# Attention in steps of two units on one Trainium2 core: products on separate halves of the array, MLA's mask in spare contraction rows

## Chip, core and metric

One core of one Trainium2 chip (trn2). The metric is the device time of one launch in microseconds (us). TensorE is PE in the profile and its weight loads are PEld; DVE is VectorE, ACT is ScalarE, POOL is GpSimd, SP is SyncE, which issues most DMAs.

## What is computed

One inference step of a layer with two head groups, for a prompt of 512 tokens and for 8 decoding sequences ("samples") of 16 new tokens with 256 cached ones. After the attention come the output projection and a retrieval layer (PEER) over 16,384 experts, which the change does not touch.

```python
def _attend(q, k, v, q_pos, k_pos, c_q, c_k, chunk_causal):
    s = jnp.einsum('bqhd,bkhd->bhqk', q, k, preferred_element_type=F32) * scale
    if c_q is not None:                      # FoX: 8 heads of 64
        s = s + (c[query] - c[key])
    if chunk_causal:                         # MLA: 8 heads of 64 + 32 rope
        mask = (k_pos[None, :] // CHUNK) <= (q_pos[:, None] // CHUNK)    # CHUNK = 64
    else:
        mask = k_pos[None, :] <= q_pos[:, None]
    s = jnp.where(mask, s, -jnp.inf)
    p = jax.nn.softmax(s, axis=-1)
    return jnp.einsum('bhqk,bkhd->bqhd', p.astype(v.dtype), v)
```

## The kernel before, in words

Everything is float32 with few exceptions (bf16 for masks and the FoX bias). The program runs through: norm and projections, transposes and MLA's up-projections, the attention stage, the output projection (L1012), PEER's queries and key scores, top-k and gate matrix, and a dense loop over 128 blocks of experts (L1117, L1133 to L1135), which takes the second half of the time.

The attention stage works on **units**. A prompt unit is one head and one tile of 128 queries, with the (i + 1) x 128 keys up to that tile; there are 32 of MLA and then 32 of FoX, ordered by pair of heads c, head hh and tile i. Between them stand 16 sample units, for each sample b one of FoX (all 8 heads x 16 queries as 128 rows, 272 keys) and one of MLA. The list `plan` (L350 to L357) writes the order out; each engine runs through it with its own lag. For a unit n:

- `scores` (L905, PE): the products into bank n % 3 of PSUM. MLA: one product over 96 rows (L924) and the mask of the diagonal block, added as identity times mask (L925). FoX: one over the head's 64 rows (L920), the bias (L921), the mask (L922). A FoX sample: four products over 128 rows, with zeros in qbd where a head doesn't belong, summed in one bank (L937), then bias and mask (L938, L939). An MLA sample: L941, L942.
- `row_max` (L1245, DVE), `exponentials` (L695, ACT), `normalise` (L1250, DVE, one unit later).
- `transpose_probabilities` (L945, PE, two units later): 128x128 blocks, into bank 3 + n % 2; `copy_transposed` (L703, ACT) brings them to SBUF.
- `values` (L955, PE, three units later): a prompt unit's products write 64 PSUM rows, the head's half (L966); a FoX sample's are 12 products with 32 moving columns (L982), an MLA sample's 3 with 128 (L985).
- `copy_out` (L1257, DVE, four units later).

So PE's program is scores(n), transposes(n - 2), values(n - 3), and so on, in order. What it waits for: scores wait for the exponentials of unit n - 3 (`exp_done`, the bank), transposes for the copy of unit n - 2 (`pt_copied`), values for their own copy.

```python
for n in range(ALL + 3):
    if n < ALL:
        scores(n)
    if 2 <= n < ALL + 2:
        transpose_probabilities(n - 2)
    if n >= 3:
        values(n - 3)
```

SP loads the caches of sample b into slot b % 2 once sample b - 2 has been used (`load_batch`, L422), w_o in between (L443). POOL writes the rope key rows of kmT (L513), zeroes and fills qbd (L516, L521), and then copies each sample's new keys (L538). After the stage, L998 up-projects the MLA samples' latents, head by head, to alternating halves of PSUM rows.

Of the kernel before, what the change touches and what calls it, by code (L numbers as in the profile page):

```python
# [36 lines left out]
P = 128  # L37
# [41 lines left out]
def peer_step_kernel(nc, t_in, t_out):  # L79
# [16 lines left out]
    with ExitStack() as ctx:  # L96
# [8 lines left out]
        eps_col = r("eps_col", [P, 8])  # L105
        late_at = r.at
# [205 lines left out]
        new_keys = sem("new_keys")  # L312
# [49 lines left out]
        def unit(n):  # L362

            m = plan[n][1]
            pair, hh, i = m // 8, m // 4 % 2, m % 4
            return 1 - pair // 4, pair % 4, hh, i, (i + 1) * P

        def keys_of(n):
            return unit(n)[4] if is_prompt(n) else L

        def batch_read(b):

            return place["sample", 2 * b + 1] + 1
# [10 lines left out]
        def _(sp):  # L384
# [54 lines left out]
            mla_read = place["prompt", UNITS // 2 - 1] + 1  # L439
            for b in range(DB):  # L440
                if b >= 2 and batch_read(b - 3 if b > 2 else 0) <= mla_read < batch_read(b - 2):
                    sp.wait_ge(pv_done, mla_read)
                    ld(w_o[:], t_in["w_o"]).then_inc(wo_loaded, 16)  # L443
                load_batch(b)
# [55 lines left out]
        def _(pool):  # L500
# [11 lines left out]
            for h in range(MH):  # L512
                nc.gpsimd.tensor_copy(kmT[64:96, h, :].rearrange("p (t k) -> p t k", t=TP),  # L513
                                      zT[64:96, 0:TP, 3, :]).then_inc(kr_copied, 1)
                pool.wait_ge(kr_copied, h + 1)
            link(nc.gpsimd.memset(qbd[:], 0.0))  # L516
            pool.wait_ge(proj_copied, 23)
            for c in range(4):
                for hh in range(2):
                    rows = slice(64 * hh, 64 * hh + 64)  # L520
                    nc.gpsimd.tensor_copy(qbd[rows, c, :, 2 * c + hh, :],  # L521
# [85 lines left out]
        def _(act):  # L607
# [87 lines left out]
            def exponentials(n):  # L695
                nk = keys_of(n)
                act.wait_ge(max_ready, n + 1)
                if n >= 4:
                    act.wait_ge(pt_done, n - 3)
                A(prob[:, n % 4, 0:nk], ps[:, n % 3, 0:nk], ACT.Exp, bias=small[:, 32 + n % 4:33 + n % 4],  # L700
                  accum_out=small[:, 36 + n % 4:37 + n % 4]).then_inc(exp_done, 1)

            def copy_transposed(n):  # L703
                act.wait_ge(pt_done, n + 1)
                if n >= 3:
                    act.wait_ge(pv_done, n - 2)
                bank = ps[:, 3 + n % 2]
                if is_prompt(n):
                    nk = keys_of(n)
                    A(probT[:, n % 3, 0:nk], bank[:, 0:nk], ACT.Copy).then_inc(pt_copied, 1)  # L710
                else:
                    A(probT[:, n % 3, 0:PAST], bank[:, 0:PAST], ACT.Copy)
                    A(probT[0:DS, n % 3, PAST:PAST + P], bank[0:DS, PAST:PAST + P], ACT.Copy).then_inc(pt_copied, 1)
# [110 lines left out]
        def _(pe):  # L824
            mm, tr = nc.tensor.matmul, nc.tensor.transpose
            identb, fmask, mmask, nmask = cb[:, 0:P], cb[:, P:2 * P], cb[:, 2 * P:3 * P], cb[:, 3 * P:3 * P + DS]
# [78 lines left out]
            def scores(n):  # L905
                bank = ps[:, n % 3]
                if n >= 3:
                    pe.wait_ge(exp_done, n - 2)
# [3 lines left out]
                if n == place["prompt", UNITS // 2]:  # L912
                    pe.wait_ge(nc_ready, 1)
                if is_prompt(n):
                    kind, c, hh, i, nk = unit(n)
                    h = 2 * c + hh
                    diag = bank[:, i * P:(i + 1) * P]
                    if kind == 0:
                        rows = slice(64 * hh, 64 * hh + 64)
                        mm(bank[:, 0:nk], fqT[rows, c, i * P:(i + 1) * P], kT[rows, c, 0:nk], start=True, stop=False)  # L920
                        mm(bank[:, 0:nk], selh[0:96, h], nc3[0:96, 0:nk], start=False, stop=False)  # L921
                        mm(diag, identb, fmask, start=False, stop=True).then_inc(s_done, 1)  # L922
                    else:
                        mm(bank[:, 0:nk], qmT[0:96, h, i * P:(i + 1) * P], kmT[0:96, h, 0:nk], start=True, stop=False)  # L924
                        mm(diag, identb, mmask, start=False, stop=True).then_inc(s_done, 1)  # L925
                    return
                b, kind = divmod(plan[n][1], 2)
                s = b % 2
                if kind == 0:
                    pe.wait_ge(batch_loaded[s], 16 * 7 * (b // 2 + 1))  # L930
                    pe.wait_ge(new_keys, 3 * (b + 1))
                    if b == 0:
                        pe.wait_ge(qbd_ready, 8)
                        pe.wait_ge(ncs_ready, 1)
                        pe.wait_ge(qs_ready, 3)
                    for c in range(4):
                        mm(bank[:, 0:L], qbd[:, c, b].rearrange("p h q -> p (h q)"), kTs[:, s, c], start=(c == 0), stop=False)  # L937
                    mm(bank[:, 0:L], selb[0:64, b], ncS[0:64], start=False, stop=False)  # L938
                    mm(bank[:, PAST:L], identb, nmask, start=False, stop=True).then_inc(s_done, 1)  # L939
                else:  # L940
                    mm(bank[:, 0:L], qps[:, b].rearrange("p h q -> p (h q)"), ckTs[:, s], start=True, stop=False)  # L941
                    mm(bank[:, 0:L], qrs[64:96, b].rearrange("p h q -> p (h q)"), krTs[64:96, s],  # L942
                       start=False, stop=True).then_inc(s_done, 1)

            def transpose_probabilities(n):  # L945
                pe.wait_ge(p_ready, n + 1)
                if n >= 2:
                    pe.wait_ge(pt_copied, n - 1)
                nk = keys_of(n)
                for c in range((nk + P - 1) // P):  # L950
                    w = min(P, nk - c * P)
                    last = tr(ps[0:w, 3 + n % 2, c * P:(c + 1) * P], prob[:, n % 4, c * P:c * P + w], ident[:])  # L952
                last.then_inc(pt_done, 1)

            def values(n):  # L955
                pe.wait_ge(pt_copied, n + 1)
                pT = probT[:, n % 3]
                if is_prompt(n):
                    kind, c, hh, i, nk = unit(n)
                    pair = plan[n][1] // 8  # L960
                    if plan[n][1] % 8 == 0 and pair >= 2:
                        pe.wait_ge(o_copied, pair - 1)
                    rows = slice(64 * hh, 64 * hh + 64)
                    for k in range(i + 1):
                        v = (fv, vm)[kind][:, k, (2 * c + hh) * 64:(2 * c + hh + 1) * 64]
                        last = mm(ps[rows, 5 + pair % 2, i * P:(i + 1) * P], v, pT[:, k * P:(k + 1) * P],  # L966
                                  start=(k == 0), stop=(k == i))
# [609 lines left out]
```

## Time and profile before

| | |
|---|---|
| median of 3 runs | 2066.52 us (2062.34 to 2066.69) |
| the profiled execution's own time | 2057.58 us |
| its span in the trace | 2055.7 us |
| PE busy over the span | 1875.9 us (91%) |
| DVE, ACT, POOL busy | 1565.2, 779.7, 913.9 us |
| mean granted TensorE clock | 0.93 |

Busy time is the union of an engine's instructions; the granted clock is given in shares of 2.4 GHz. A line such as `L966` is a line of the kernel, `128*64` the stationary operand (rows x columns), `128x128` the moving one. A float32 product shows as two instructions, a transpose as one. The duration of one instruction holds its latency too, so what a row of them costs is read from start to start.

### The profile page before, as it was taken

The numbers are of one execution on the slowest core, as the hardware profiler recorded it, in microseconds if no ns is written. First come the engines' busy times: TensorE is split into PE (matmuls) and PEld (weight loads), VectorE is DVE, ScalarE is ACT, GpSimd is POOL, SyncE is SP. The second block draws the span as 40 slices with busy tenths as digits, with TensorE's granted clock in tenths as the row PEclk, the third lists the DMA queues.
The fourth block names the chain that finished last, engine by engine and source line by source line (L and its number), as shares of the span: only waits on it lengthen the run. The fifth ranks groups of instructions, "written<-read, shape, count | busy, mean of one in ns | idle before, by whom it ended". The sixth has DMA issues, their size and how long they took to land.

```text
span 2055.7 us, 28703 instructions
## 1 busy us (share of the span) xinstructions
PE 1875.9 (91%) x9135; PEld 1519.7 (74%) x9135; DVE 1565.2 (76%) x3265; ACT 779.7 (38%) x1298; POOL 913.9 (44%) x727
## 2 busy tenths in 40 slices
PE   6999999999989952665799999999999999999998
PEld 4883666664555642664799999999999999999997
DVE  4314333332267989996799999999999999999999
ACT  4322432220211112995344344443444344443443
POOL 0011000000004445001477777777777777777772
PEclk8999877779999875999999999999999999999999
DMA  6110212102111002445899999999999999999994
GB/s 235 42 61 0 82 55 112 52 1 114 41 41 42 21 1 80 176 181 205 327 415 407 397 408 405 409 403 399 414 413 397 394 399 417 416 392 413 405 413 194
DMA packets 159300, 502.54 MB, mean 244 GB/s; under 512 B 17776, under 2 KB 51504, under 8 KB 155536
## 3 DMA queue, kind: packets, MB, share of 16 engines
q0 software_dynamic: 73728, 268.47, 32.7%
q1 hardware_dynamic: 85520, 233.42, 29.5%
q8 instruction: 27, 0.44, 0.1%
q14 instruction: 25, 0.20, 0.0%
HBM read 470.99 MB, written 30.84 MB: 244 GB/s over the span
## 4 chain that ended last, share of the span: by engine, by line
PE 84%; DVE 12%; ACT 2%; issue 1%; DMA 1%; SPq 0%; DVEq 0%; ACTq 0%
PE ps L1117 25%; PE ps L1133 9%; PE ps L1134 9%; PE ps L1135 9%; PE ps L1036 6%; DVE asel L1417 4%; PE ps L1012 3%; PE ps L966 3%; DVE bsel L1409 3%; PE ps L854 2%; PE ps L855 2%; PE ps L856 2%; PE ps L920 2%; PE ps L982 2%; PE ps L952 2%; PE ps L1043 1%
## 5 line engine op out<-in xcount | busy, mean ns | idle before, releaser
L543 POOL DMA_INDIRECT vbuf<-in_peer_v,ix x256 | 381.0, 1488 | 221.6 <-DMA gate_matrix<-stage 143.9
L543 POOL DMA_INDIRECT ubuf<-in_peer_u,ix x256 | 383.3, 1497 | 156.0 <-POOL ix L598 108.9
L1133 PE MATMUL ps<-hh,uh 128*128 128x384 f32 x1024 | 346.2, 338 | 10.7 <-DVE ul L1158 10.7
L1134 PE MATMUL ps<-hl,uh 128*128 128x384 f32 x1024 | 345.0, 337 | 0.0
L1135 PE MATMUL ps<-hh,ul 128*128 128x384 f32 x1024 | 344.8, 337 | 0.0
L1441 DVE SCALAR_TENSOR_TENSOR ubuf<-ubuf,h 128x1024 f32<-128x1024 f32 x256 | 302.2, 1217 | 1.1 <-issue 1.1
L1117 PE MATMUL ps<-vh,acth 128*128 128x512 f32 x774 | 238.5, 389 | 0.0
L1117 PE MATMUL ps<-vl,acth 128*128 128x512 f32 x774 | 238.3, 389 | 0.0
L1117 PE MATMUL ps<-vh,actl 128*128 128x512 f32 x774 | 238.3, 389 | 0.0
L800 ACT ACTIVATE vh<-vb 128x1024 fp32r<-128x1024 f32 x128 | 136.1, 1063 | 242.9 <-PE ps L1117 242.7
L1133 PEld LDWEIGHTS ps<-hh,uh 128*128 128x128 f32 x1024 | 193.2, 189 | 16.2 <-DVE ul L1158 11.1
L1134 PEld LDWEIGHTS ps<-hl,uh 128*128 128x128 f32 x1024 | 193.2, 189 | 5.1 <-issue 0.2
L1135 PEld LDWEIGHTS ps<-hh,ul 128*128 128x128 f32 x1024 | 193.2, 189 | 0.0
L565 POOL TENSOR_TENSOR onehot<-onehot,i16f 128x2560 f32<-128x2560 f32 x7 | 48.6, 6940 | 318.3 <-DVE onehot L1374 318.3
L1158 DVE TENSOR_TENSOR vl<-vb,vh 128x1024 fp32r<-128x1024 f32 x128 | 155.9, 1218 | 23.6 <-ACT vh L800 23.6
L1247 DVE TENSOR_REDUCE small<-ps 128x1 f32<-128x128 f32 (+4 forms) x80 | 38.5, 481 | 173.8 <-PE ps L922 59.7
L1117 PEld LDWEIGHTS ps<-vl,acth 128*128 128x128 f32 x774 | 145.3, 188 | 30.5
L1117 PEld LDWEIGHTS ps<-vh,actl 128*128 128x128 f32 x774 | 145.3, 188 | 30.2
L1461 DVE SCALAR_TENSOR_TENSOR x<-vbuf,wts,x 128x1024 f32 x128 | 163.7, 1279 | 0.0
L1465 DVE SCALAR_TENSOR_TENSOR x<-vbuf,wts,x 128x1024 f32 x128 | 163.4, 1276 | 0.0
L1158 DVE TENSOR_TENSOR ul<-ub,uh 128x1024 fp32r<-128x1024 f32 x129 | 156.8, 1215 | 4.8 <-ACT uh L790 4.8
L1117 PEld LDWEIGHTS ps<-vh,acth 128*128 128x128 f32 x774 | 143.5, 188 | 20.2
(289 smaller groups left out, 3049.7 us busy)
## 6 DMA issues: line engine op xcount, KB each, us to landing
ub<-in_peer_uT SPq DMA_DIRECT2D x129, 512.0 KB, 6.9
vb<-in_peer_v SPq DMA_DIRECT2D x128, 512.0 KB, 6.9
gate_matrix<-stage SPq DMA_DIRECT2D x12, 2048.0 KB, 6.3
gbuf<-gate_matrix SPq DMA_DIRECT2D x64, 384.0 KB, 11.2
wpq<-in_wpq SPq DMA_DIRECT2D x8, 1024.0 KB, 4.9
kTs<-in_past_k SPq DMA_DIRECT2D x8, 512.0 KB, 4.2
vs<-in_past_v SPq DMA_DIRECT2D x8, 512.0 KB, 4.9
w_o<-in_w_o SPq DMA_DIRECT2D x1, 4096.0 KB, 12.8
```

What stands on the lines that cost most here:

```text
L543: nc.gpsimd.indirect_dma_start(out=dst[:, slot, e, :], out_offset=None, in_=t_in[table], in_offset=bass.IndirectOffsetOnAxis(ix[:, slot, e ...
L800: A(vh[:, s % 2], vb[:, s], ACT.Copy).then_inc(vh_ready, 1)
L1036: mm(ps[:, c], wpq[:, h % 2, k, c * P:(c + 1) * P], h2T[:, k, 0:SEQ], start=(k == 0), stop=(k == KD - 1))
L1117: ins = mm(ps[:, 2 * d + half], a[:, d * P:(d + 1) * P], v[:, half * 512:(half + 1) * 512], start=False, stop=last_block and n == 2, skip_ ...
L1133: mm(ps[:, 6 + slot, 0:NTD], uh[:, slot, k], hh[:, k], start=(k == 0), stop=False)
L1134: mm(ps[:, 6 + slot, 0:NTD], uh[:, slot, k], hl[:, k], start=False, stop=False)
L1135: last = mm(ps[:, 6 + slot, 0:NTD], ul[:, s, k], hh[:, k], start=False, stop=(k == KD - 1))
L1158: V.tensor_tensor(low, full, high.bitcast(F32), ALU.subtract).then_inc(done, 1)
L1417: ins = V.tensor_scalar(asel[:, q, k], iota[:], i1T[:, tok:tok + 1], gT[:, tok:tok + 1], ALU.is_equal, ALU.mult)
L1441: ins = V.scalar_tensor_tensor(out=ubuf[:, s, e], in0=ubuf[:, s, e], scalar=1.0, in1=row(h2), op0=ALU.mult, op1=ALU.mult, accum_out=dots[: ...
L1461: V.scalar_tensor_tensor(out=row(x2), in0=vbuf[:, s, 0], scalar=wts[:, s, 0:1], in1=row(x2), op0=ALU.mult, op1=ALU.add).then_inc(half_done, 1)
L1465: V.scalar_tensor_tensor(out=row(x2), in0=vbuf[:, s, 1], scalar=wts[:, s, 1:2], in1=row(x2), op0=ALU.mult, op1=ALU.add).then_inc(acc_done, 1)
```

## The change

A step of `plan` now holds two units: both heads of a pair for one tile (32 steps), or both kinds of a sample (8 steps). The tiles of a pair come in the order 3, 0, 2, 1. Units still take score banks in turn (three), now two per step; exponentials are signalled per unit; transposes of the two units go to banks 3 and 4, with one copy for both. Probabilities have six buffers, transposed ones two (of two units each). FoX's two 64-row score products stand next to each other, one on rows 0 to 63, one on 64 to 127. Value products alternate between the two heads, so between PSUM rows 0 to 63 and 64 to 127. A FoX sample's four score products each write 32 rows of the bank, and qbd shrinks to two heads per pair. MLA's mask is in the product: rows 96 to 99 of qmT hold, for the first 64 queries of tile i, a one in row 96 + i; the same rows of kmT hold -1e30 at the last 64 keys of tile i. POOL fills these rows before the stage. The sample's value products are as before, the two kinds in one step.

```diff
-        prob = a2("prob", [P, 4, SEQ])
-        probT = a2("probT", [P, 3, SEQ])
-        qbd = a2("qbd", [P, 4, DB, FH, DS])
+        prob = a2("prob", [P, 6, SEQ])
+        probT = a2("probT", [P, 2, 2, SEQ])
+        qbd = a2("qbd", [P, 4, DB, 2, DS])
...
-        UNITS, SAMPLES = 64, 2 * DB
         plan = []
-        for m in range(UNITS):
-            plan.append(("prompt", m))
-            plan += [("sample", k) for k in range(SAMPLES) if 8 + 7 * k // 2 == m + 1]
+        for m in range(32):
+            plan.append(("mla" if m < 16 else "fox", m % 16 // 4, (3, 0, 2, 1)[m % 4]))
+            plan += [("sample", b, 0) for b in range(DB) if 5 + 7 * b // 2 == m + 1]
         ALL = len(plan)
-        assert ALL == UNITS + SAMPLES
-        place = {unit_: n for n, unit_ in enumerate(plan)}
-        def is_prompt(n):
-            return plan[n][0] == "prompt"
-        def unit(n):
-            m = plan[n][1]
-            pair, hh, i = m // 8, m // 4 % 2, m % 4
-            return 1 - pair // 4, pair % 4, hh, i, (i + 1) * P
+        assert ALL == 32 + DB
+        place = {step: n for n, step in enumerate(plan)}
+        FOX_START, MLA_STOP = place["fox", 0, 3], place["mla", 3, 1] + 1
         def keys_of(n):
-            return unit(n)[4] if is_prompt(n) else L
+            kind, _, i = plan[n]
+            return L if kind == "sample" else (i + 1) * P
+        def pair_of(n):
+            kind, c, _ = plan[n]
+            return (kind == "fox") * 4 + c
...
+            first, second = ([x.rearrange("p h (i k) -> p h i k", i=TP)[:, :, :, y * 64:(y + 1) * 64]
+                              for x in (qmT[96:96 + TP, :, 0:SEQ], kmT[96:96 + TP])] for y in range(2))
+            tile_of = ident[96:96 + TP, 96:96 + TP].unsqueeze(1).unsqueeze(3).broadcast_to([TP, MH, TP, 64])
+            nc.gpsimd.memset(second[0], 0.0).then_inc(mask_rows, 1)
+            pool.wait_ge(mask_rows, 1)
+            nc.gpsimd.memset(first[1], 0.0).then_inc(mask_rows, 1)
+            pool.wait_ge(mask_rows, 2)
+            nc.gpsimd.tensor_copy(first[0], tile_of).then_inc(mask_rows, 1)
+            pool.wait_ge(mask_rows, 3)
+            nc.gpsimd.tensor_scalar(second[1], tile_of, NEG, None, ALU.mult).then_inc(mask_rows, 1)
+            pool.wait_ge(mask_rows, 4)
...
-                act.wait_ge(max_ready, n + 1)
-                if n >= 4:
-                    act.wait_ge(pt_done, n - 3)
-                A(prob[:, n % 4, 0:nk], ps[:, n % 3, 0:nk], ACT.Exp, bias=small[:, 32 + n % 4:33 + n % 4],
-                  accum_out=small[:, 36 + n % 4:37 + n % 4]).then_inc(exp_done, 1)
+                if n >= 3:
+                    act.wait_ge(pt_done, n - 2)
+                for u in (2 * n, 2 * n + 1):
+                    act.wait_ge(max_ready, u + 1)
+                    A(prob[:, u % 6, 0:nk], ps[:, u % 3, 0:nk], ACT.Exp, bias=stat[:, 0, u % 6:u % 6 + 1],
+                      accum_out=stat[:, 1, u % 6:u % 6 + 1]).then_inc(exp_done, 1)
...
-                if n >= 3:
-                    act.wait_ge(pv_done, n - 2)
-                bank = ps[:, 3 + n % 2]
-                if is_prompt(n):
+                if n >= 2:
+                    act.wait_ge(pv_done, n - 1)
+                if plan[n][0] != "sample":
                     nk = keys_of(n)
-                    A(probT[:, n % 3, 0:nk], bank[:, 0:nk], ACT.Copy).then_inc(pt_copied, 1)
+                    A(probT[:, n % 2, :, 0:nk], ps[:, 3:5, 0:nk], ACT.Copy).then_inc(pt_copied, 1)
...
             def scores(n):
-                bank = ps[:, n % 3]
-                if n >= 3:
-                    pe.wait_ge(exp_done, n - 2)
+                banks = [ps[:, (2 * n + x) % 3] for x in range(2)]
+                if n >= 1:
+                    pe.wait_ge(exp_done, 2 * n - 1)
...
+                if kind == "mla":
+                    for x in range(2):
+                        mm(banks[x][:, 0:nk], qmT[0:96 + TP, 2 * c + x, i * P:(i + 1) * P], kmT[0:96 + TP, 2 * c + x, 0:nk],
+                           start=True, stop=True).then_inc(s_done, 1)
                     return
...
+                if kind == "fox":
+                    for x in range(2):
+                        rows = slice(64 * x, 64 * x + 64)
+                        mm(banks[x][:, 0:nk], fqT[rows, c, i * P:(i + 1) * P], kT[rows, c, 0:nk], start=True, stop=False)
+                    for x in range(2):
+                        mm(banks[x][:, 0:nk], selh[0:96, 2 * c + x], nc3[0:96, 0:nk], start=False, stop=False)
+                        mm(banks[x][:, i * P:nk], identb, fmask, start=False, stop=True).then_inc(s_done, 1)
+                    return
...
+                for c in range(4):
+                    mm(banks[0][32 * c:32 * c + 32, 0:L], qbd[:, c, b].rearrange("p h q -> p (h q)"), kTs[:, s, c],
+                       start=True, stop=False)
+                mm(banks[0][:, 0:L], selb[0:64, b], ncS[0:64], start=False, stop=False)
...
             def transpose_probabilities(n):
                 pe.wait_ge(p_ready, n + 1)
-                if n >= 2:
-                    pe.wait_ge(pt_copied, n - 1)
+                if n >= 1:
+                    pe.wait_ge(pt_copied, n)
                 nk = keys_of(n)
-                for c in range((nk + P - 1) // P):
-                    w = min(P, nk - c * P)
-                    last = tr(ps[0:w, 3 + n % 2, c * P:(c + 1) * P], prob[:, n % 4, c * P:c * P + w], ident[:])
+                for x in range(2):
+                    for k in range((nk + P - 1) // P):
+                        w = min(P, nk - k * P)
+                        last = tr(ps[0:w, 3 + x, k * P:(k + 1) * P], prob[:, (2 * n + x) % 6, k * P:k * P + w], ident[:])
...
-                        last = mm(ps[rows, 5 + pair % 2, i * P:(i + 1) * P], v, pT[:, k * P:(k + 1) * P],
-                                  start=(k == 0), stop=(k == i))
+                        for x in range(2):
+                            v = (vm if kind == "mla" else fv)[:, k, (2 * c + x) * 64:(2 * c + x + 1) * 64]
+                            last = mm(ps[64 * x:64 * x + 64, 5 + pair % 2, i * P:(i + 1) * P], v, pT[:, x, k * P:(k + 1) * P],
+                                      start=(k == 0), stop=(k == i))
                     last.then_inc(pv_done, 1)
...
+                for u in (2 * n, 2 * n + 1):
+                    dve.wait_ge(s_done, u + 1)
+                    V.tensor_reduce(stat[:, 0, u % 6:u % 6 + 1], ps[:, u % 3, 0:keys_of(n)], AX.X, ALU.max,
+                                    negate=True).then_inc(max_ready, 1)
...
+                dve.wait_ge(exp_done, 2 * n + 2)
+                x = 2 * n % 6
+                link(V.reciprocal(stat[:, 1, x:x + 2], stat[:, 1, x:x + 2]))
+                for x in (x, x + 1):
+                    pr = prob[:, x, 0:keys_of(n)]
+                    ins = V.tensor_scalar(pr, pr, stat[:, 1, x:x + 1], None, ALU.mult)
+                ins.then_inc(p_ready, 1)
```

## Rows read from the trace of the kernel before

**Rows 1.** The page, section 2: TensorE's granted clock in 40 slices, in tenths.
```profile
PEclk8999877779999875999999999999999999999999
```

**Rows 2.** Windows: stage, then stretches; busy by engine, clock, DMA share, GB/s.
```profile
206.73:461.60 254.87, 250.38 (x1129) 162.28 (x1129) 84.67 (x273) 80.79 (x260) 5.00 (x24) 0.77 0.18 61
212.74:219.57 6.83, 6.83 (x24) 4.62 (x25) 2.21 (x9) 2.94 (x9) 0.00 (x0) 0.50 0.88 288
219.57:236.64 17.07, 17.07 (x99) 11.84 (x98) 6.61 (x21) 5.62 (x19) 0.00 (x0) 1.00 0.01 1
403.89:427.78 23.89, 23.89 (x76) 14.89 (x76) 5.22 (x18) 4.81 (x16) 0.00 (x0) 0.50 0.00 1
441.44:451.68 10.24, 10.24 (x38) 6.87 (x38) 2.85 (x11) 3.00 (x10) 0.00 (x0) 0.50 0.00 1
```

**Rows 3.** Who waited for whom in the stage: total us, times, longest.
```profile
PEld ps L952 <- DVE prob L1255: 5.3, 8, 2.7
```

**Rows 4.** Timeline of TensorE, MLA units at the upper level: start, duration, instruction.
```profile
228.41 0.70 PE L924 MATMUL ps<-kmT,qmT 96*128 96x256 f32 x2
228.95 0.22 PE L925 MATMUL ps<-cb 128*128 128x128 bf16 x1
229.01 0.49 PE L952 MATMUL ps<-ident,prob 128*128 128x128 f32 x3
229.44 1.09 PE L966 MATMUL ps<-probT,vm 128*64 128x128 f32 x8
230.45 0.91 PE L924 MATMUL ps<-kmT,qmT 96*128 96x384 f32 x2
231.20 0.22 PE L925 MATMUL ps<-cb 128*128 128x128 bf16 x1
```

**Rows 5.** The same, one FoX unit of 256 keys.
```profile
390.87 0.70 PE L920 MATMUL ps<-kT,fqT 64*128 64x256 f32 x2
391.49 0.28 PE L921 MATMUL ps<-nc,selh 96*128 96x256 bf16 x1
391.61 0.22 PE L922 MATMUL ps<-cb 128*128 128x128 bf16 x1
391.67 0.60 PE L952 MATMUL ps<-ident,prob 128*128 128x128 f32 x4
392.21 0.87 PE L966 MATMUL ps<-probT,fv 128*64 128x128 f32 x6
393.01 2.10 PE L937 MATMUL ps<-kTs,qbd 128*128 128x272 f32 x8
```

**Rows 6.** The same, MLA unit at the lower level.
```profile
239.06 0.85 PE L952 MATMUL ps<-ident,prob 128*128 128x128 f32 x3
239.84 1.12 PE L966 MATMUL ps<-probT,vm 128*64 128x128 f32 x4
```

**Rows 7.** Chain of waits in the stage: start, us, value products of a FoX sample.
```profile
231.54 3.38 PE ps L982 x24
...
402.25 5.06 PE ps L982 x24
```

**Rows 8.** Timeline of TensorE at the stage's end: the up-projection.
```profile
459.64 1.09 PE L998 MATMUL ps<-latT,w_uv 128*64 128x128 f32 x13
```

**Rows 9.** Groups by shape in the stage, VectorE and ScalarE, 384 and 512 keys.
```profile
L1247 DVE TENSOR_REDUCE small<-ps 128x1 f32<-128x384 f32 x16 | 8.9, 557 | 33.7 <-PE ps L922 20.1 <-PE ps L925 13.6
...
L710 ACT ACTIVATE probT<-ps 128x512 f32<-128x512 f32 x16 | 9.4, 590 | 0.9 <-PE ps L952 0.8
L700 ACT ACTIVATE prob<-ps,small 128x384 f32<-128x384 f32 x16 | 9.3, 582 | 36.8 <-DVE small L1247 36.8
```

**Rows 10.** POOL: its wait before the first sample's keys, and the fill.
```profile
POOL kTs L538 <- ACT qrs L691: 47.4, 1, 47.4
...
L516 POOL MEMSET qbd<- 128x4096 f32 x1 | 3.7, 3676 | 0.1
```

**Rows 11.** The page, section 6: a batch's key load, us to landing.
```profile
kTs<-in_past_k SPq DMA_DIRECT2D x8, 512.0 KB, 4.2
```

More of the change, by code:

```diff
@@ L520, in _ @@
                     rows = slice(64 * hh, 64 * hh + 64)
-                    nc.gpsimd.tensor_copy(qbd[rows, c, :, 2 * c + hh, :],
+                    nc.gpsimd.tensor_copy(qbd[rows, c, :, hh, :],
                                           fqT[rows, c, SEQ:NT].rearrange("p (b q) -> p b q", b=DB)).then_inc(qbd_ready, 1)
@@ L911, in scores @@
                     pe.wait_ge(kr_copied, MH)
-                if n == place["prompt", UNITS // 2]:
+                    pe.wait_ge(mask_rows, 4)
+                if n == FOX_START:
                     pe.wait_ge(nc_ready, 1)
[L914 to L925, printed above, removed]
-                    return
@@ L927, in scores @@
[L927 to L943, printed above, removed]
+                kind, c, i = plan[n]
@@ L956, in values @@
                 pe.wait_ge(pt_copied, n + 1)
[L957 to L961, printed above, removed]
+                pT = probT[:, n % 2]
+                kind, c, i = plan[n]
+                if kind != "sample":
+                    pair = pair_of(n)
+                    if i == 3 and pair >= 2:
                         pe.wait_ge(o_copied, pair - 1)
-                    rows = slice(64 * hh, 64 * hh + 64)
@@ L968, in values @@
                     last.then_inc(pv_done, 1)
                     return
-                m = plan[n][1]
-                b, kind = divmod(m, 2)
-                s = b % 2
-                if m >= 1:
-                    pe.wait_ge(so_copied, m)
-                bank = ps[:, 7]
-                for c in range(4 if kind == 0 else 1):
+                b, s = c, c % 2
+                if b >= 1:
+                    pe.wait_ge(so_copied, b)
+                for c in range(4):
                     for k in range(3):
@@ L978, in values @@
                         rows = slice(0, P if k < 2 else DS)
[L979 to L985 removed]
+                        v = vs[:, s, k, c * P:(c + 1) * P] if k < 2 else vn[0:DS, s, c * P:(c + 1) * P]
@@ L986, in values @@
+                        mm(ps[:, 7, 32 * c:32 * c + 32], v, pT[rows, 0, k * P + 32 * c:k * P + 32 * c + 32],
+                           start=(k == 0), stop=(k == 2))
+                for k in range(3):
+                    rows = slice(0, P if k < 2 else DS)
+                    v = ckr[:, s, k] if k < 2 else ckn[0:DS, s]
+                    last = mm(ps[:, 7, P:2 * P], v, pT[rows, 1, k * P:(k + 1) * P], start=(k == 0), stop=(k == 2))
                 last.then_inc(pv_done, 1)
@@ new lines, in normalise @@
+                dve.wait_ge(exp_done, 2 * n + 2)
[5 more added lines that the diff above has]
+                ins.then_inc(p_ready, 1)
+            def copy_out(n):
+                kind, c, i = plan[n]
+                if kind != "sample":
+                    if i == 1:
+                        dve.wait_ge(pv_done, n + 1)
+                        V.tensor_copy(oT[:, 4 * (kind == "mla") + c, 0:SEQ], ps[:, 5 + pair_of(n) % 2]).then_inc(o_copied, 1)
+                    return
+                dve.wait_ge(pv_done, n + 1)
+                new = slice(SEQ + c * DS, SEQ + (c + 1) * DS)
+                for x in range(2):
+                    rows = slice(64 * x, 64 * x + 64)
+                    V.tensor_copy(oT[rows, 0:4, new],
+                                  ps[rows, 7, 0:P].rearrange("p (c x) -> p c x", c=4)[:, :, DS * x:DS * x + DS])
+                V.tensor_copy(latT[:, :, c * DS:(c + 1) * DS],
+                              ps[:, 7, P:2 * P].rearrange("p (h q) -> p h q", h=MH)).then_inc(so_copied, 1)
```

68 lines of the change are left out of this document (24 added, 44 removed).

## The prediction

> **What bounds the kernel now.** I read the clock line of the page first. It falls below full speed in slices 5 to 9 [rows 1], while the slices after slice 20 stand at the top: the first place to look is the attention stage. The window view gives that stage, from the first score product (206.73 us) to the last value product (461.60 us), 254.87 us; TensorE (PE) is busy 250.38 of them, VectorE and ScalarE a third of them each [rows 2]. So TensorE ends the stage, and its granted clock is 0.77 on average. The waits agree: the longest wait of TensorE's weight loads for another engine's result is 5.3 us in total [rows 3]. TensorE's time here is worth its full amount in the result; VectorE's, ScalarE's and POOL's is worth nothing until they become late.
>
> The same windows show the clock as two levels: stretches at 2.4 GHz (1.00) and at 1.2 GHz (0.50), with TensorE 99 to 100% busy in both [rows 2]. A mean of 0.77 means (1 - 0.77)/0.5 = 46% of the stage, 117 us, at the lower level; I count nine such stretches, of 6.8 to 23.9 us (the first, the longest and the last stand there). Eight of them begin 1.6 to 5.1 us after the start of the 24 narrow value passes of a FoX sample (L982, 32 moving columns each) [rows 2, 7], the ninth in the slow start of the stage.
>
> **Prices at 2.4 GHz.** A float32 product is two instructions ("passes") in the trace; a transpose is one. The distance from one group's start to the next is what it costs. MLA unit with 256 keys: score product 0.54 us, mask 0.06; 384 keys 0.75 [rows 4]; each 128 columns more are 0.21, so the mean over the four tile sizes is 0.645. Three transposes take 0.43 [rows 4], four 0.54 [rows 5]: 0.11 each and 0.10 fixed. Eight value passes take 1.01, six 0.80: 0.105 each and 0.17 fixed [rows 4, 5]. FoX scores cost 0.62 at 256 keys, so 0.73 on average, the bias product 0.12, its mask 0.06 [rows 5]. Twice 320 columns at 0.21/256 us is 0.53, so the fixed part is 0.11 for an MLA score and 0.20 for a FoX one. Those fixed parts stand where the shape of the stationary operand changes (96, 64 or 128 rows, 64 or 128 columns).
>
> At 1.2 GHz three transposes take 0.78 [rows 6] against 0.43, 1.8 times as long. The L982 block of 402.25 us takes 5.06 instead of 3.38; it ran 1.64 us before the clock fell at 403.89 and 3.42 after, in which it did 1.74 us of work, 2.0 times [rows 2, 7]. I take 1.85 over the stage: of each us at the lower level 0.46 us is lost. The stage's work at 2.4 GHz is then 254.9 - 0.46 x 117 = 201.1 us.
>
> **The change, part by part (us at 2.4 GHz).**
> - MLA's mask product goes: 32 x 0.06 = 1.9. The score product has 100 instead of 96 rows and the same columns; FoX at 64 rows pays the same per column [rows 4, 5], so the four rows cost nothing.
> - Steps of two units: the fixed parts are paid once per pair. MLA 0.11 + 0.10 + 0.17 = 0.38, times 16 = 6.1. FoX 0.20 + 0.10 + 0.17 = 0.47, times 16 = 7.5. A sample's two kinds share one change between scores and one before the next step, about 0.3, times 8 = 2.4.
> - Value products alternate between the array's column halves. The up-projection L998 does this already: 13 passes in 1.09 us, less 0.27 for the last one's own latency, are 12 distances of 0.068 [rows 8] against 0.105. 320 passes x 0.037 = 11.8. Bounds: 0, and 320 x 0.052 = 16.6 if two ran fully at once. I take the row of the same shape.
> - FoX score products on the two row halves. No row shows row halves together. Instructions go in order and each head's two passes are adjacent, so only the first head's second pass can meet the second head's first: three pass lengths of 0.267 instead of four, 16 x 0.267 = 4.3. Bounds: 0 and 8.5.
> - A FoX sample's four products go to four column strips of 32 instead of being summed over 128: by the same order five passes of 0.23 instead of eight (all eight are the last of [rows 5], 2.10 us). 3 x 0.23 x 8 = 5.4; bounds 0 and 10.9.
> Sum 39.4, so 161.7 us of work remain. Edits at zero: the number of transposes, of L982's narrow products and of exponentials is unchanged.
> - The row halves have a price in the Trainium skill: "TensorEngine Tiling (Array Packing)", section "Performance Considerations", promises twofold for a contraction of 64. By it the FoX term is 8.5 rather than 4.3, the result 4 to 5 us lower; no trace here shows it.
>
> POOL gets four fills of 2,048 columns on four partitions and loses three quarters of the qbd fill. At that fill's 3.68 us for 4,096 columns it is +7.4 - 2.8 = 4.6 us, and twice that if copies are dearer. It lies ahead of the first score, where POOL then waits 47.4 us for ScalarE [rows 10]: nothing. SP's order of loads is the same; a batch's loads still start when the batch before last has been used, five steps ahead (some 20 us), and land in 4.2 us [rows 11]. Behind SP's wait stand only the next batch and w_o.
>
> New waits: scores of a step wait for the first exponential of the step before (three banks for two units); transposes wait for the copy of the step before (one pair of banks). For 384 keys: after a step's first score, VectorE needs 0.557 twice and ScalarE 0.582 twice plus a copy of 768 columns, some 0.8 [rows 9]: the copy ends about 2.2 us after the scores. TensorE has its transposes 0.76, values 0.99 and next scores 1.39, 3.1 us, ahead of the waiting transposes. About 0.9 us of cover, so zero. If it is gone, the queue behind is all of TensorE's stage.
>
> **The clock decides how 39.4 is multiplied.** The stage lasts 161.7 + 0.46 t, t being the time at 1.2 GHz. The L982 blocks remain, all eight, and so does the start: I keep nine falls. With 13 us each as before, t = 117 and the stage is 215.5 (-39.4). But the early stretches, among MLA steps, were 6.8, 6.8, 10.2 and 13.7 us, the later ones, among FoX's 64-row products, mostly 17 to 24. The change fills the idle halves in FoX steps and shortens what lies between, so I take 10.5 us each: t = 94.5, stage 205.2, 50 us less. With 6.8 each t = 61 and the gain is 65; with the upper bounds of the row term (+4) and the strips (+5) about 74.
>
> The profiled execution took 2057.58 us for a span of 2055.7, 8.9 below the median of 2066.52. Taken from the median: 2066.5 - 50 = 2016 (from the profiled execution's own time it would be 2008).
>
> **Rivals.**
> - No side by side (chance 0.10): halves run one after the other, so 21.5 of the 39.4 vanish; about 18 remain at full speed, 23 with the clock's share (t = 106): 2044. L998 speaks against it for columns, nothing for rows.
> - The waits bind (0.08): if VectorE and ScalarE react later than the sum above, about 0.7 us at each of 40 steps, 28 us are given back: 2044, or some 2035 if only at full clock. Against: the 0.9 us of cover; for: both buffers are thinner than before.
> - Slower: the clock stays down (0.05). With overlapped products TensorE streams less of the time, short waits add to it, and 1.2 GHz holds through the stage: 161.7 x 1.85 = 299, +44: 2111. It decides from t = (254.9 - 161.7)/0.46 = 203 us, a mean granted clock of about 0.60. For it: TensorE fell to 0.50 while 100% busy. Against: each time it came back, among the same steps that now become denser.
> - The clock stays up (0.02). The rows show falls with TensorE fully busy [rows 2]. If it fell only for idle gaps, the stage would be 162 us: 1973. "TensorE: Matmul & The Clock Gate", Part 1 of the Trainium skill, names idleness as what brings the lower level; the trace disagrees, hence 0.02.
> - My forecast: 0.75.
>
> **How the numbers follow.** The likeliest case gives 2016, its own range 1998 to 2030. Downwards I keep 1997; upwards 2044 takes in the two rivals that give back half. That leaves out some 0.2. The waits' 0.08 is divided, 0.06 still faster and 0.02 no change, if the cover is far thinner than summed. Faster by over 0.2% (about what a measurement of this kernel can tell from no change): 0.75 + 0.10 + 0.06 + 0.02 = 0.93; within it 0.02; slower 0.05.
>
> **What would show it.** Stage from first score to last value near 205 us, mean clock near 0.77, TensorE still over 95% busy; value passes at 0.07 us; FoX score pairs at three pass lengths; L982 block still followed by the lower level. Wrong if value passes stand at 0.105, if TensorE waits more than some 15 us for ScalarE's copies or exponentials, or if the mean clock is under 0.65.

## The result and the profile after

The changed kernel takes 1987.27 us in the median of 5 runs (1985.23 to 1997.39), against 2062.34 us for 5 runs of the kernel before: ratio 0.9645, 95% interval [0.9619, 0.9671]. Some 75 us are gained where 50 were forecast, and the time lies 10 us below the lower end of the range. The direction was right; the size was not. The profiled execution is the slowest of the five, 1997.39 us for a span of 1995.6 us.

Windows of the changed kernel: the attention stage (first score product to the start of the output projection), then its first stretch at the lower level and the next one at the upper. The columns are those of [rows 2].

```profile
207.70:393.30 185.60, 180.30 (x1098) 120.43 (x1097) 77.48 (x233) 76.11 (x212) 4.96 (x24) 0.79 0.25 83
211.54:218.37 6.83, 6.27 (x18) 4.56 (x19) 3.21 (x10) 3.33 (x12) 0.00 (x0) 0.50 1.02 332
218.37:238.85 20.48, 20.40 (x157) 14.16 (x155) 10.73 (x31) 10.86 (x32) 0.21 (x1) 1.00 0.08 23
```

The stage went from 254.9 to 185.6 us. TensorE is still busy 97% of it, so it still sets the end. The clock's mean hardly moved, 0.77 to 0.79, but the stage is shorter: there are nine stretches at 1.2 GHz again, now 78.5 us in all instead of 119.5 (both summed from the stretches of the trace).

TensorE's waits for others in the stage (all those over 1 us) answer to [rows 3]; the columns are total, times, longest.

```profile
PEld ps L928 <- ACT prob L710: 3.9, 4, 2.8
PE ps L928 <- ACT prob L710: 2.4, 2, 1.9
...
PEld ps L934 <- ACT prob L710: 1.5, 8, 0.2
PE ps L963 <- ACT probT L722: 1.3, 2, 0.6
```

They stay under 10 us together, and TensorE itself stands idle for 5.3 us of the stage, against 4.5 before. The thinner buffers cost next to nothing.

Timeline of TensorE in the changed kernel: a sample's strips, a block of value products with 512 keys, and a FoX step with 256 keys. It answers to [rows 4, 5].

```profile
223.47 0.67 PE L947 MATMUL ps<-kTs,qbd 128*32 128x272 f32 x8
224.07 0.72 PE L949 MATMUL ps<-ncS,selb 64*128 64x272 f32 x2
...
231.69 1.09 PE L977 MATMUL ps<-probT,vm 128*64 128x128 f32 x16
232.71 0.48 PE L928 MATMUL ps<-kmT,qmT 100*128 100x256 f32 x1
...
307.80 0.70 PE L934 MATMUL ps<-kT,fqT 64*128 64x256 f32 x4
308.44 0.28 PE L936 MATMUL ps<-nc,selh 96*128 96x256 bf16 x1
```

This is where the forecast went wrong. Sixteen value passes take 1.02 us from start to start; eight took 1.01 in [rows 4]. Four FoX score passes take 0.64 us; two took 0.62 in [rows 5]. The sample's eight passes take 0.60 us instead of 2.04. In the single records the four strips start 7 ns apart, and the four second passes follow 0.25 us after them. Two halves cost what one did, and the four strips run 3.4 times as fast as their sum did. "TensorEngine Tiling (Array Packing)", section "Overview", of the Trainium skill gives up to twofold for a dimension of at most 64 and up to fourfold for one of at most 32. For float32 products of two passes each the trace reaches the twofold, and 3.4 of the fourfold.

The narrow value products of a FoX sample are as before (chain of waits, changed kernel). A stretch at 1.2 GHz begins 2.1 to 5.2 us after the start of each of the eight blocks, once inside the block and seven times behind it:

```profile
234.06 3.38 PE ps L988 x24
...
315.23 4.26 PE ps L988 x24
...
380.76 3.38 PE ps L988 x24
```

**The change also costs some 6 us where it touches nothing.** Between the two traced executions the span fell by 60 us, the stage by 69. Most of the rest lies in the loop over the experts. Its products (L1117, now L1125) are the same, but take 389 ns each before and 391 to 392 after (behind the first bar, the busy time in us and the mean ns of one):

```profile
L1117 PE MATMUL ps<-vh,acth 128*128 128x512 f32 x774 | 238.5, 389 | 0.0
...
L1125 PE MATMUL ps<-vh,acth 128*128 128x512 f32 x774 | 240.9, 392 | 0.0
```

The loop, from its first product to its last, takes 1072.9 and 1071.5 us in the two traces of the kernel before (one of them with the edits of a later experiment) and 1077.9 to 1082.6 us in the twelve of the changed kernel and its variants. No run here shows why. So the lengths of the stage, and not the times of whole kernels, are compared below when the kernel before and the changed one stand side by side.

### The profile page after: what moved, and what is told of

It is laid out like the page before. It is cut to its first block, busy times and chain, and to the rows that moved or that the text cites. A ratio compares the mean times of both kernels' runs of the same rounds, so it can differ in the third digit from the quotient of the medians.

```text
span 1995.6 us, 28371 instructions
## 1 busy us (share of the span) xinstructions
PE 1816.5 (91%) x9103; PEld 1479.4 (74%) x9103; DVE 1557.1 (78%) x3225; ACT 768.4 (39%) x1250; POOL 906.7 (45%) x731
## 4 chain that ended last, share of the span: by engine, by line
PE 82%; DVE 12%; ACT 2%; issue 2%; DMA 1%; SPq 0%; DVEq 0%; ACTq 0%
PE ps L1125 25%; PE ps L1141 9%; PE ps L1142 9%; PE ps L1143 9%; PE ps L1044 6%; DVE asel L1425 4%; PE ps L1020 3%; DVE bsel L1417 3%; PE ps L863 2%; PE ps L864 2%; PE ps L865 2%; PE ps L963 2%; PE ps L1051 1%; PE ps L988 1%; PE ps L977 1%
## 5 line engine op out<-in xcount | busy, mean ns | idle before, releaser
L552 POOL DMA_INDIRECT vbuf<-in_peer_v,ix x256 | 373.8, 1460 | 221.6 <-DMA gate_matrix<-stage 143.9
L552 POOL DMA_INDIRECT ubuf<-in_peer_u,ix x256 | 371.4, 1451 | 156.4 <-POOL ix L607 109.3
L1141 PE MATMUL ps<-hh,uh 128*128 128x384 f32 x1024 | 346.3, 338 | 10.5 <-DVE ul L1166 10.4
L1125 PE MATMUL ps<-vh,acth 128*128 128x512 f32 x774 | 240.9, 392 | 0.0
L1125 PE MATMUL ps<-vh,actl 128*128 128x512 f32 x774 | 239.8, 391 | 0.0
L1125 PE MATMUL ps<-vl,acth 128*128 128x512 f32 x774 | 239.7, 391 | 0.0
L809 ACT ACTIVATE vh<-vb 128x1024 fp32r<-128x1024 f32 x128 | 135.7, 1060 | 154.1 <-PE ps L1125 153.5
L1125 PEld LDWEIGHTS ps<-vl,acth 128*128 128x128 f32 x774 | 145.3, 188 | 32.8
L1125 PEld LDWEIGHTS ps<-vh,actl 128*128 128x128 f32 x774 | 145.2, 188 | 31.7
L1125 PEld LDWEIGHTS ps<-vh,acth 128*128 128x128 f32 x774 | 143.5, 188 | 21.7
L1108 PE MATMUL ps<-asel,bsel 128*128 128x128 f32 x768 | 100.4, 285 | 46.3 <-DVE asel L1425 46.3
```

The costliest lines, as they stand in the source:

```text
L552: nc.gpsimd.indirect_dma_start(out=dst[:, slot, e, :], out_offset=None, in_=t_in[table], in_offset=bass.IndirectOffsetOnAxis(ix[:, slot, e ...
L809: A(vh[:, s % 2], vb[:, s], ACT.Copy).then_inc(vh_ready, 1)
L1108: last = mm(ps[:, g, k * P:(k + 1) * P], bsel[:, q, tok], asel[:, q, tok], start=True, stop=True)
L1125: ins = mm(ps[:, 2 * d + half], a[:, d * P:(d + 1) * P], v[:, half * 512:(half + 1) * 512], start=False, stop=last_block and n == 2, skip_ ...
L1141: mm(ps[:, 6 + slot, 0:NTD], uh[:, slot, k], hh[:, k], start=(k == 0), stop=False)
```

## The experiments

Two measures are used besides the time: the length of the stage, and its **work**, the length less 0.46 of its time at 1.2 GHz (the prediction's conversion). Work is 199.9 us before and 149.5 after the change. Each length and work is from one traced execution.

**One part undone at a time.** First the value products, one head after the other:

```diff
-                    for k in range(i + 1):
-                        for x in range(2):
+                    for x in range(2):
+                        for k in range(i + 1):
```

> The changed kernel with one edit: the two heads' value products one head after the other instead of alternating. Theory A (the two column halves run fully at once: starts 7 ns apart in the changed kernel's trace, one pair per 0.109 us): passes go back to 0.107 us each, 320 x 0.054 = 17 us of work at 2.4 GHz, 17 to 30 us of time over the changed kernel with the clock's share. Theory B (my forecast's, only every other pass overlaps, 0.068 us a pass): 12 us of work, 12 to 20 us of time. If column halves were worth nothing: no change.

It took 1993.20 us, ratio to the kernel before 0.9668 [0.9614, 0.9722], which can't be told from the changed kernel; work 154.5 us, 5 more. Neither theory gave that. The timeline tells why:

```profile
227.44 0.67 PE L977 MATMUL ps<-probT,vm 128*64 128x128 f32 x8
228.03 0.59 PE L928 MATMUL ps<-kmT,qmT 100*128 100x384 f32 x1
...
230.17 1.58 PE L977 MATMUL ps<-probT,vm 128*64 128x128 f32 x16
231.68 0.48 PE L928 MATMUL ps<-kmT,qmT 100*128 100x256 f32 x1
```

Eight passes, four of each head, still take 0.59 us, as in the changed kernel (0.58). Sixteen take 1.51, between 1.02 (side by side) and the 1.85 that 16 distances of 0.105 and the fixed 0.17 would give. The records do not name the head, but two rows of eight passes can be told by their distance of 0.109 us, and the second row begins 6 ns after the first row's fifth pass, though it stands behind its eighth in the program. So the edit did not take the halves apart: passes for the free half overtake those that wait for the busy one. The trace of the kernel before shows the same with the lines named, at the end of the stage: L998 stands behind all of L966 in the program, and its first pass starts ahead of the last three of L966 (two of them stand here).

```profile
459.26 0.32 PE L998 MATMUL ps<-latT,w_uv 128*64 128x128 f32 x1
459.36 0.27 PE L966 MATMUL ps<-probT,fv 128*64 128x128 f32 x1
459.42 0.27 PE L998 MATMUL ps<-latT,w_uv 128*64 128x128 f32 x1
459.47 0.27 PE L966 MATMUL ps<-probT,fv 128*64 128x128 f32 x1
```

The experiment measures this, and not the worth of alternating.

Next, FoX's two 64-row products with the bias and the mask between them:

```diff
                         mm(banks[x][:, 0:nk], fqT[rows, c, i * P:(i + 1) * P], kT[rows, c, 0:nk], start=True, stop=False)
-                    for x in range(2):
                         mm(banks[x][:, 0:nk], selh[0:96, 2 * c + x], nc3[0:96, 0:nk], start=False, stop=False)
```

> The changed kernel with one edit: FoX's bias and mask of a head follow its own 64-row product, so the two row halves no longer stand next to each other. Theory A (row halves fully at once): two more pass lengths per step, 16 x 0.533 = 8.5 us, and two more changes of shape per step, 16 x 0.30 = 5 us: 13 us of work at 2.4 GHz, 13 to 22 us of time. Theory B (three pass lengths out of four): 4.3 + 5 = 9 us of work, 9 to 15 of time. If the row halves ran one after the other: 5 us.

2020.35 us (2006.26 to 2037.04), ratio 0.9765 [0.9684, 0.9845] without the slowest run; work 159.7 us, 10 more. The runs lie in two groups, 2006 and 2008, and 2033 and 2037. The profiled one is the slowest, and the windows of its FoX part show what that is:

```profile
309.69:326.76 17.07, 17.07 (x120) 10.94 (x119) 7.46 (x21) 7.03 (x22) 0.00 (x0) 1.00 0.61 247
326.76:418.92 92.16, 92.16 (x350) 53.54 (x350) 24.05 (x72) 23.48 (x63) 1.25 (x6) 0.50 0.10 31
```

92 us in one piece at 1.2 GHz with TensorE busy throughout. It is not the price of the edit: the mean granted clock of the upper two runs is 0.925 and 0.927, but 0.942 in both lower ones, as in the changed kernel (0.938 to 0.946 in nine runs). The lower two are 14 to 20 us above the changed kernel's medians at the same clock, within theory A's 13 to 22. The price was measured again below with the clock out of the way.

The sample's strips, back to zeros and a sum over 128 columns:

```diff
-        qbd = a2("qbd", [P, 4, DB, 2, DS])
+        qbd = a2("qbd", [P, 4, DB, FH, DS])
...
-                    mm(banks[0][32 * c:32 * c + 32, 0:L], qbd[:, c, b].rearrange("p h q -> p (h q)"), kTs[:, s, c],
-                       start=True, stop=False)
+                    mm(banks[0][:, 0:L], qbd[:, c, b].rearrange("p h q -> p (h q)"), kTs[:, s, c],
+                       start=(c == 0), stop=False)
```

> The changed kernel with one edit: a FoX sample's four score products are again over 128 columns of stationary operand with zeros, summed in the bank. Theory A (four strips start together, so two pass lengths in place of eight): 6 x 0.23 x 8 = 11 us of work at 2.4 GHz, 11 to 17 of time. Theory B (five pass lengths): 5.4 us of work, 5 to 9 of time.

1996.18 us, ratio 0.9694 [0.9633, 0.9755]; work 162.4, 13 more (theory A had 11, B 5.4), but only 44.4 us at 1.2 GHz in the profiled execution, so its stage is 182.8 us, no longer than the changed kernel's. More work, less of it at the lower level: the time alone would have hidden the price.

MLA's mask as a product again (the indices of the operands are cut):

```diff
-                        mm(banks[x][:, 0:nk], qmT[0:96 + TP, ...], kmT[0:96 + TP, ...],
-                           start=True, stop=True).then_inc(s_done, 1)
+                        mm(banks[x][:, 0:nk], qmT[0:96, ...], kmT[0:96, ...],
+                           start=True, stop=False)
+                        mm(banks[x][:, i * P:nk], identb, mmask, start=False, stop=True).then_inc(s_done, 1)
```

> The changed kernel with MLA's mask as a product of its own again (32 products of 0.06 us at 2.4 GHz): all theories 2 us more work, 2 to 4 us of time. A rival that would surprise: the 100-row product itself costs or gives something, then the MLA score distances differ from 0.215 us a pass at 256 columns.

1994.55 us, ratio 0.9658 [0.9602, 0.9715]; work 151.7, 2.2 more. As expected in work; the time can't tell it from none. The passes of 256 columns are 0.22 us apart with 96 rows and with 100, so the four mask rows are free.

All four undone, so that the pairing alone stays:

> Steps of two units alone: value products one head after the other, FoX score products apart, the sample's four products summed, MLA's mask a product again. Theory A (side by side is worth 17 + 8.5 + 11 us of work, the mask 2, the rest is the pairing): the work left of the gain is 10 to 16 us at 2.4 GHz, so 2062 - (12 to 22) = 2040 to 2050 us. Theory B (side by side is worth only 21 of the gain and the clock does the rest): 2025 to 2035 us. Rival (the pairing itself keeps TensorE's clock up): under 2025 us, with less than 85 us of the stage at 1.2 GHz.

2027.41 us, ratio 0.9806 [0.9749, 0.9863]. The time lies where theory B put it, the work does not: 180.4 us, 19.5 under the kernel before (theory A had 10 to 16). The first experiment explains it: the value products of this kernel still run side by side in part, and cost 28.2 us where they cost 44.5 before. That is 16 of the 19.5, so the pairing gave only some 3 us elsewhere. The time at 1.2 GHz is 78.5 us, 41 less than before the change, which is the rest of the gain. The rival, that the pairing itself keeps the clock up, had asked for less than 85 us there and a time under 2025. The first came true and the second was missed by 2 us: the changed kernel has no less time at 1.2 GHz than this one, so by these two traces its gain by the clock came with the pairing, or with what still overlaps here, and needs none of the other parts.

**What brings the clock down.** Every stretch but the first begins at the narrow value products or just behind them. They were changed in two ways: 96 moving columns instead of 32 (64 of them unused), and the key blocks outermost, so that the four products over 16 rows stand together. The columns of the bank and the copies out of it move along; these lines are cut here.

```diff
-                        mm(ps[:, 7, 32 * c:32 * c + 32], v, pT[rows, 0, k * P + 32 * c:k * P + 32 * c + 32],
+                        first = k * P + 32 * (c == 3)
+                        mm(ps[:, 7, 96 * c:96 * c + 96], v, pT[rows, 0, first:first + 96],
...
```

> The changed kernel with one edit: the 12 value products of a FoX sample move 96 columns instead of 32 (64 of them are not used), so the same number of passes at the same distance (0.112 us, set by the 128-column weight load) stream three times the columns. Theory C (the narrow products bring TensorE's clock down): the stretches at 1.2 GHz that begin at these blocks vanish or shorten, from 79 us to under 35, and the time falls by 12 to 25 us against the changed kernel. Theory D (the clock falls for another reason in the sample's steps, its waits or shape changes): no change within 4 us.

1980.06 us, ratio 0.9585 [0.9535, 0.9634]; 44.4 us at 1.2 GHz, in five stretches instead of nine. Work is 153.5, 4 more, since the block of 24 passes now takes 3.81 us instead of 3.38; the same distance had been expected. The time at 1.2 GHz fell by less than theory C forecast, and the kernel gained more than D allows.

```diff
-                for c in range(4):
-                    for k in range(3):
+                for k in range(3):
+                    for c in range(4):
...
-                           start=(k == 0), stop=(k == 2))
+                           start=(k == 0 and c == 0), stop=(k == 2), skip_group_check=True)
```

> The changed kernel with the sample's 12 value products ordered by key block first, so that the four products over 16 rows stand together: the stationary operand's row count changes twice instead of eight times. The block of 24 passes goes from 3.38 to about 2.8 us, 8 x 0.6 = 5 us of work. Theory C: the narrow stretch is shorter, so the clock falls a little less often: 5 to 12 us. Theory D (shape changes bring the clock down): most of the falls vanish, 15 to 30 us.

1979.36 us, ratio 0.9586 [0.9537, 0.9635]; work 144.0, 5 less, as forecast; 58.0 us at 1.2 GHz in eight stretches. The falls did not vanish, so the shape changes alone are not their cause.

Both edits together:

> Both edits together. Theory C: as the first alone plus 5 us, 17 to 30 us below the changed kernel. Theory D: as the second alone.

1962.45 us, ratio 0.9492 [0.944, 0.9544]. It is faster than with either edit alone, and 25 us below the changed kernel's median, which is in theory C's range. Windows of its stage:

```profile
207.96:357.10 149.14, 143.42 (x1097) 98.55 (x1096) 78.39 (x249) 75.76 (x212) 5.01 (x24) 0.98 0.31 104
```

Only the 6.8 us of the start are left at the lower level. The block of 24 passes takes 2.82 us; it is shorter and streams three times the columns, and no fall follows it in this trace. The mean granted clock of the four runs, 0.955 to 0.960 against 0.938 to 0.946 in nine of the changed kernel, says the same of the executions that were not traced. Which matters, the columns, the grouping or the shorter block, is not separated by these runs.

The same two edits in the kernel before the change:

> The kernel before the change with the two edits of the last experiment (96 moving columns, key block outermost) in its FoX sample value products. If the narrow products are what brings the clock down there too, the stage falls from 255 us to 200 to 210 us with less than 30 us at 1.2 GHz: 2008 to 2020 us, 45 to 55 less. Rival (in the kernel before the 64-row products and half-filled arrays keep the clock down by themselves): 5 us of work and little more, 2045 to 2060 us.

```profile
207.40:409.50 202.10, 197.07 (x1129) 130.05 (x1128) 85.92 (x289) 80.26 (x260) 5.01 (x24) 0.97 0.22 77
```

2007.88 us, ratio 0.9721 [0.9683, 0.976], with 10.2 us at 1.2 GHz. The two edits took the stage of the kernel before from 254.9 to 202.1 us, 53 us: 50 are the clock (109.2 us fewer at 1.2 GHz, times 0.46) and 2.5 are work. With the clock up in both, the change takes the stage from 202.1 to 149.1 us, also 53. The medians of the two kernels are only 45 us apart, and the loop over the experts, 8.7 us longer in the second, accounts for the difference.

The changed kernel once more:

> The changed kernel itself once more, for a second trace. Both theories: 1985 to 1997 us; the work of the stage, length less 0.46 of its time at 1.2 GHz, again 149 us within 3, and the time at 1.2 GHz between 50 and 80 us: if the executions differ by the clock alone, the difference in length of the two stages is 0.46 of the difference in that time.

1992.61 us, ratio 0.9666 [0.9631, 0.9701]; stage 181.9 us, 71.7 of them at 1.2 GHz, work 148.9. Between its two traces the stage differs by 3.7 us, and 0.46 of the difference at the lower level is 3.1.

**Prices with the clock up.** The row halves and the strips were undone in the changed kernel with both edits, whose stage is 149.1 us. First the row halves:

> The kernel with both edits of the sample's value products, whose clock stays up, and in it FoX's two row halves apart. Measured against that kernel (stage 149.2 us). Theory A (row halves fully at once): 8.5 + 2 to 5 = 10 to 13 us. Theory B (three pass lengths of four): 6 to 9 us. If a long stretch at 1.2 GHz in the FoX part comes back as in the second experiment, the halves side by side hold the clock up by themselves, and it is 25 us or more.

```profile
206.70:372.00 165.30, 160.91 (x1098) 104.91 (x1097) 79.78 (x249) 77.64 (x212) 5.01 (x24) 0.95 0.28 94
```

1973.30 us, ratio 0.9579 [0.9545, 0.9612]. The stage is 16.2 us longer. 10.2 us more are at 1.2 GHz, which is 4.7 of it; 11.5 are work, in theory A's 10 to 13. The long stretch did not return. But two short ones did, of 10.2 and 3.4 us, each 5 us after the start of a widened block and one of them among the MLA steps, where the two programs are alike: the widened and grouped block makes the falls rare, not impossible.

Then the strips:

> The same kernel with a FoX sample's four score products summed over 128 columns. Theory A (four strips at once): 11 us longer in the stage. Theory B (five pass lengths): 5.4 us.

```profile
207.90:368.60 160.70, 154.90 (x1098) 108.85 (x1097) 78.39 (x249) 75.63 (x212) 4.97 (x24) 0.98 0.29 96
```

1971.09 us, ratio 0.9549 [0.9518, 0.958]; the stage is 11.6 us longer with the same 6.8 us at 1.2 GHz. That is theory A's 11, not theory B's 5.4.

## Why the prediction was wrong, and where it was right

The step that failed is the sentence "Instructions go in order and each head's two passes are adjacent, so only the first head's second pass can meet the second head's first", and with it "I take the row of the same shape" for the value passes. It sized the three side-by-side terms at half to seven tenths of their upper bounds; the measured values are near the bounds. The runs showed in its place that two halves run fully at once (4 passes in 0.64 us where 2 took 0.62, and 16 in 1.02 where 8 took 1.01), because a pass for a free half does not wait for its turn in the program.

The table sets the forecast terms beside what TensorE spent on each product in the two kernels whose clock stayed up, the one before and the changed one, each with the two edits (distances from each pass's start to the next, summed over the stage; passes at 1.2 GHz divided by 1.85).

| us at 2.4 GHz | before | changed | gain | forecast |
|---|---|---|---|---|
| FoX first score product | 23.5 | 11.9 | 11.6 | 4.3 + 3.2 fixed |
| sample's four products | 16.2 | 4.8 | 11.4 | 5.4 |
| value products of the prompt | 44.6 | 23.0 | 21.6 | 11.8 + 5.4 fixed |
| masks, the samples' too | 6.6 | 3.8 | 2.8 | 1.9 |
| transposes | 32.1 | 26.4 | 5.7 | 3.2 fixed |
| MLA score product | 20.4 | 22.6 | -2.2 | 1.8 fixed |
| the samples' other shape changes | | | 0 | 2.4 |
| all of the stage | 197.4 | 146.0 | 51.4 | 39.4 |

Point by point:
- **TensorE bounds the stage, before and after**: right. VectorE, ScalarE and POOL at zero: right; TensorE's waits were under 10 us, and the rival of the binding waits is refuted.
- **Side by side**: the mechanism was right, the size off by 14 us in the three terms together. The 0.068 us of [rows 8] misled: in the single records the first nine distances of that row are 0.054 us on average and the last three 0.109, because at the end only one half had passes left. A mean over both is no steady state. The ends of the row term (8.5) and of the strips (10.9) had been written down; the values in the middle came from an argument about order that no row bore out, and that the lines 459.26 to 459.47 of the same trace, just ahead of [rows 8], spoke against.
- **Pairing**: 16 us forecast for fixed parts. It is not seen by itself; the fixed parts of the FoX scores and value products are in the rows above, the transposes gave 2.5 more than forecast, the MLA scores and the samples 6.4 less. The MLA score product did not get slower: in the changed kernel 2.8 of its 22.6 us are TensorE standing idle behind it, and in the kernel before such waits stand behind the masks (1.9 us, and 1.3 after). Without the idle time the score gained 0.6 us and the masks 2.2.
- **The clock**: nine falls, mean clock near 0.77, and the narrow block before each but the first: right. That the stretches would be 10.5 us each was a choice between values, and they were 8.7 and 8.0. 94.5 us at 1.2 GHz were forecast, 78.5 and 71.7 measured, which is 7 to 10 us of the error. The rest, some 12, is the table's difference. The stage was forecast at 205.2 and came to 185.6 and 181.9. Another 4 us of the miss in the kernel's time are the starting point: the forecast counted from 2066.5, and the kernel before measured 2062.34.
- **The rest of the program**: it was put at nothing without a word, and the loop over the experts became some 6 us longer. By luck this hid a part of the error.
- **The twofold of the Trainium skill** ("TensorEngine Tiling (Array Packing)", section "Overview") for a contraction of 64 was the better price: 8.5, with the fixed part 11.7; measured 11.6.
- **"The clock stays up"** as a rival had the wrong ground (idle gaps), and the last experiments show that it can be had.

Of the 69 to 73 us that the stage lost, about 51 are work; the other 19 to 22 are time at 1.2 GHz that the shorter stage no longer has (119.5 less 78.5 or 71.7 us, times 0.46). Why that time fell along with the work is not shown; it was 78.5 us with the pairing alone, too.

## What to carry to other kernels

Where a float32 product leaves half of the array's rows or columns idle, put the other head's product next to it on the other half and count the pair as one, not as three quarters. Look at the clock line before counting instructions: a few narrow products per step held this stage at 1.2 GHz for almost half of its time, and widening what they move, at no more passes, and grouping equal shapes gave back as much in the kernel before as the whole change's work. Judge a small edit by work and by time at each clock level apart, since the same edit can add to one and take from the other, and look at the parts of the program that were not touched as well.

## What the runs showed of the hardware that was not expected

- Passes on a free half of the array overtake earlier ones in the program. With the heads one after the other, 8 value passes took 0.59 us (0.58 alternating) and 16 took 1.51 us (1.02 alternating). "TensorE: Matmul & The Clock Gate", Part 3, of the Trainium skill says that matmuls keep the order of the program; these traces disagree for passes on different halves. In the kernel before, a pass of L998 starts at 459.26 us and one of L966, which stands ahead of it, at 459.36.
- The clock fell with TensorE busy, each time but the first at or just behind 24 passes of 32 columns: 78.5 us at 1.2 GHz. In the 8 us before each of these eight falls TensorE had no idle time at all, or in two cases 0.64 us of it. With 96 columns it was 44.4 us, with fewer shape changes 58.0, with both 6.8, and 10.2 with both in the kernel before.
- A stretch at the lower level can be long: 92.2 us in one piece in the trace where FoX's row halves stood apart and the narrow block was in place, and none longer than 10.2 us in the four traces where the block was widened and grouped. Two of that kernel's four runs had no such stretch by their mean clock, and no run tested what starts one.
- A loop that an edit does not touch can change: the experts' products took 389 ns in both traces of the kernel before and 391 to 392 in all twelve of the changed one and its variants. The cause is open.
